# A two-block transformer kernel: branch projections by seven products per pair of output tiles

## The reference

```python
branches = jnp.stack([o_a, o_b, o_c, o_d], axis=2)                       # [1, 512, 4, 512]
up = jnp.einsum("bsnc,ncd->bsnd", branches, w_branch[l])                 # w_branch[l]: [4, 512, 1024]
gates = jax.nn.sigmoid((h @ w_gate[l]).reshape(bsz, seq, N_BRANCH, D_MODEL))
mix = jnp.einsum("bsnd,bsnd->bsd", gates, up) @ w_o[l]
x = x + rms_norm_2(mix, norm_mix_post[l])
```

## Time and profile before

| | us |
|---|---|
| median of 3 runs | 4093.86 |
| the profiled execution, whole | 4087.29 |
| its span, first to last instruction | 4085.5 |
| TensorE busy | 3939.4 (96%) |
| VectorE busy | 2078.0 (51%) |
| GpSimd busy | 1321.1 (32%) |
| ScalarE busy | 828.2 (20%) |

### The profile page before, as it was taken

One profiled execution on the slowest core, in us unless ns is written; L12 is line 12 of the kernel. 1 busy time (PEld: TensorE's weight loads), 2 busy tenths in 40 slices (PEclk: granted clock), 3 DMA queues, 4 the chain that ended last, 5 costly groups with the idle time before them and its releaser, 6 DMA issues. The chain is left out here.

```text
span 4085.5 us, 56674 instructions
## 1 busy us (share of the span) xinstructions
PE 3939.4 (96%) x21187; PEld 3094.6 (76%) x21187; DVE 2078.0 (51%) x3906; ACT 828.2 (20%) x1862; POOL 1321.1 (32%) x1044
## 2 busy tenths in 40 slices
PE   7997999999998999999999999999999999999998
PEld 3886768887886688866688648888666887478887
DVE  3776344423653333225648336884364486257852
ACT  2442310002333100014401202111143201011110
POOL 1333224443320244421146102454311372004543
PEclk8999999999998999999999999999999999999999
DMA  7322234325341233362233231332522233313322
GB/s 240 77 62 94 67 110 130 86 85 162 110 124 39 80 87 84 92 128 41 53 79 89 72 92 52 90 85 85 114 62 65 55 84 82 93 42 93 87 83 77
DMA packets 623320, 360.86 MB, mean 88 GB/s; under 512 B 69083, under 2 KB 592764, under 8 KB 622629
## 3 DMA queue, kind: packets, MB, share of 16 engines
q1 hardware_dynamic: 607960, 335.62, 30.5%
q10 hardware_dynamic: 15180, 22.80, 1.7%
HBM read 344.21 MB, written 6.82 MB: 86 GB/s over the span
## 5 line engine op out<-in xcount | busy, mean ns | idle before, releaser
L851 PE MATMUL psum<-h_normed,weight_slot 128*128 128x256 f32 x2624 | 593.8, 379 | 0.0
L851 PEld LDWEIGHTS psum<-h_normed,weight_slot 128*128 128x128 f32 x2624 | 498.6, 190 | 68.6 <-issue 1.0
L759 POOL TENSOR_TENSOR weight_slot<-weight_slot 128x512 f32<-128x512 f32 (+1 forms) x130 | 170.7, 1313 | 879.5 <-DMA weight_slot<-in_w_ffn_in 292.1
L951 DVE COPY work<-psum 128x256 f32<-128x256 f32 x98 | 41.3, 422 | 592.5 <-PE psum L851 592.4
L3630 PE MATMUL psum<-sums_of_h,weight_slot 128*128 128x256 f32 x1280 | 282.8, 379 | 0.0
L3630 PEld LDWEIGHTS psum<-sums_of_h,weight_slot 128*128 128x128 f32 x1280 | 243.2, 190 | 33.1
L851 PE MATMUL psum<-sums_hidden,weight_slot 128*128 128x256 f32 x1056 | 243.7, 379 | 0.5 <-POOL weight_slot L765 0.5
L851 PE MATMUL psum<-sums_in,weight_slot 128*128 128x256 f32 x1008 | 231.3, 379 | 0.0
L851 PE MATMUL psum<-sums_of_h,weight_slot 128*128 128x256 f32 x960 | 220.5, 379 | 3.7 <-POOL weight_slot L765 3.7
L4522 DVE SCALAR_TENSOR_TENSOR u<-raw,vectors,u 128x511 f32<-128x511 f32 (+1 forms) x160 | 192.2, 1221 | 60.1 <-ACT u L4494 48.4
L3630 PE MATMUL psum<-h_normed,weight_slot 128*128 128x256 f32 x960 | 217.6, 383 | 5.2 <-PEq L209 5.2
(11 more groups left out here) (605 smaller groups left out, 7018.7 us busy)
## 6 DMA issues: line engine op xcount, KB each, us to landing
weight_slot<-in_w_ffn_in SPq DMA_DIRECT2D x88, 512.0 KB
weight_slot<-in_ffn_w_up SPq DMA_DIRECT2D x88, 512.0 KB
weight_slot<-in_w_gate SPq DMA_DIRECT2D x64, 512.0 KB
weight_slot<-in_w_in SPq DMA_DIRECT2D x40, 512.0 KB, 5.4
weight_slot<-in_dsw_w_in SPq DMA_DIRECT2D x36, 512.0 KB, 6.6
weight_slot<-in_gdn_w_in SPq DMA_DIRECT2D x32, 512.0 KB, 14.5
weight_slot<-in_w_ffn_out SPq DMA_DIRECT2D x64, 256.0 KB
tile_ahead<-in_w_ada SPq DMA_DIRECT2D x16, 1024.0 KB, 5.3
```

What stands on the lines that cost most here:

```text
L759: nc.gpsimd.tensor_tensor(b(self.S1), b(self.A21), b(self.A22), ALU.add).then_inc(self.folded, 1)
L851: last = nc.tensor.matmul(c.ps[:, 4 * bank + r // 2, (r % 2) * self.HALF:(r % 2 + 1) * self.HALF], c.slots[s][:, b * 512 + k * P:b * 512 + ...
L951: nc.vector.tensor_copy(u4, p(self.P1)).then_inc(self.link, 1)
```

## The change

Instead of 8 output tiles, `merge_branches` runs 16 steps: 4 pairs of output tiles (i and i + 4) by 4 branches, in the branch order 0, 3, 2, 1. Each step is a 2 x 2 block product with half a branch's depth (256 channels) and half the positions (256) to a block, by seven products; a product has 2 k-tiles. The steps are written out, not looped.

- Folds S2 to S4 are made like S1 in the diff below, each waiting for the one before it; the input sums t2 = b22 - t1, t3 = b22 - b12 (in place of b12) and t4 = b21 - t2 follow t1 in one chain too.
- Weights: 4 buffers of half a slot; two DMAs of 256 KB a step. The first two loads are issued at the end of `conv_pool_gates`, where one of 1 MB was.
- GpSimd: folds each step's weights (4 operations, 128 x 256), makes the input sums (4 operations, 128 x 512) of branches 0 and 3 at the end of `conv_pool_gates` together with the first two folds, those of branch 2 in `merge_branches`, and adds each gated branch to the sum of its pair (2 operations, 128 x 512), 11 of the 12 times.
- VectorE: input sums of branch 1, seven operations per step to combine, two products with the gates, and the last pair of additions.
- ScalarE: copies P1 in each step.
- w_o is loaded in four pairs of tiles as buffers come free, and the first two half products leave k-tiles 3 and 7 for the end.
- New room: `made` (two pairs of tiles) and `work`; input sums lie in `shared` and in `c.h`.

```diff
-def conv_pool_gates(c, layer, o_conv, o_pool, gates, sums_in):
+def conv_pool_gates(c, layer, o_conv, o_pool, gates, sums_in, early):
...
+        ahead = BranchProducts(c, c.next_sems(), early, None)
...
         @block.gpsimd
...
             pool.sem_inc(pooled, 1)
+            pool.wait_ge(done, 2 + SEVEN)
+            for b in EARLY:
+                ahead.sum_inputs(pool, nc.gpsimd, b)
+            for n in range(2):
+                ahead.fold(pool, n)
...
         @block.sync
...
             sp.wait_ge(done, STEPS + 1)
-            sp.dma_start(branch_tile(c, 0), branch_weights(c, layer, 0)).then_inc(c.next_sems()[LOAD0], 16)
+            for n in range(2):
+                ahead.load(sp, layer, n)
...
+BRANCHES = (0, 3, 2, 1)
+EARLY = BRANCHES[0:2]
+
+class BranchProducts(SevenSteps):
+    KB = BW // 2
+    BUFFERS = 4
+    STEPS = KT // 2 * len(BRANCHES)
...
+    def buffer(self, n):
+        m = n % self.BUFFERS
+        at = (1 - m % 2) * (SLOT // 2)
+        return self.c.slots[m // 2][:, at:at + SLOT // 2]
...
+    def fold(self, pool, n):
+        b = lambda j: self.block(n, j)
+        pool.wait_ge(self.loaded[n % self.BUFFERS], 32 * (n // self.BUFFERS + 1))
+        nc.gpsimd.tensor_tensor(b(self.S1), b(self.A21), b(self.A22), ALU.add).then_inc(self.folded, 1)
+        pool.wait_ge(self.folded, 4 * n + 1)
...
+    def sum_inputs(self, engine, on, b):
+        b11, b12, b21, b22 = self.quarters(b)
+        t1, t2, t4 = (self.operands[b][1][:, j, :, :] for j in range(3))
+        on.tensor_tensor(t1, b12, b11, ALU.subtract).then_inc(self.summed[b], 1)
...
+    def multiply(self, pe, n):
...
+        pe.wait_ge(self.loaded[n % self.BUFFERS], 32 * (n // self.BUFFERS + 1))
+        if n >= 2:
+            pe.wait_ge(self.combined, 4 * n - 4)
+        for r, weights, name in ORDER:
+            if r == self.P6:
+                pe.wait_ge(self.folded, 4 * n + 4)
+                if n < len(BRANCHES):
+                    pe.wait_ge(self.summed[b], 4)
+            for k in range(BW // P // 2):
+                last = nc.tensor.matmul(c.ps[:, 4 * (n % 2) + r // 2, (r % 2) * self.HALF:(r % 2 + 1) * self.HALF],
+                                        self.block(n, weights)[:, k * P:(k + 1) * P], self.operand(b, name, k),
+                                        start=(k == 0), stop=(k == BW // P // 2 - 1))
...
 def merge_branches(c, layer, operands, gates, late_room):
...
         @block.gpsimd
...
+            def add_branch(n):
+                if n % NB == 0:
+                    return
+                before = 2 * (n - n // NB - 1)
+                pool.wait_ge(gated, 2 * n + 2)
+                if before:
+                    pool.wait_ge(added, before)
+                for g in range(2):
+                    sum_ = gates[:, n // NB + g * (KT // 2), :]
+                    nc.gpsimd.tensor_tensor(sum_, sum_, made[:, n % 2, g, :], ALU.add).then_inc(added, 1)
+
+            seven.fold(pool, 2)
+            seven.sum_inputs(pool, nc.gpsimd, BRANCHES[2])
+            seven.fold(pool, 3)
+            for n in range(1, STEPS):
+                add_branch(n - 1)
+                if n + 3 < STEPS:
+                    seven.fold(pool, n + 3)
             tail.add_pool(pool, range(KT))
...
         @block.scalar
...
+            for n in range(STEPS):
+                seven.copy_first(act, n)
...
         @block.sync
+            for n in range(2, STEPS):
+                if n >= seven.BUFFERS:
+                    sp.wait_ge(seven.done, n - seven.BUFFERS + 1)
+                seven.load(sp, layer, n)
+            for buffer, q in enumerate((0, 2, 1, 3)):
+                sp.wait_ge(seven.done, STEPS - seven.BUFFERS + buffer + 1)
+                for n in (2 * q, 2 * q + 1):
+                    sp.dma_start(out_tile(c, n), layer_columns(c.ins["w_o_2"], layer, n * P, P)).then_inc(out_loaded[q], 16)
...
         @block.tensor
...
+            for n in range(STEPS):
+                seven.multiply(pe, n)
...
+            LAST_MADE = (KT // 2 - 1, KT - 1)
+            READY = tuple(k for k in range(KT) if k not in LAST_MADE)
+            pe.wait_ge(out_loaded[0], 32)
+            pe.wait_ge(seven.combined, 4 * (STEPS - 1))
+            product(0, READY)
+            product(1, READY)
+            product(0, LAST_MADE)
+            product(1, LAST_MADE)
...
         @block.vector
+            seven.sum_inputs(dve, nc.vector, BRANCHES[3])
+            for n in range(STEPS):
+                i, b = n // NB, BRANCHES[n % NB]
+                if n >= 2 and (n - 2) % NB:
+                    dve.wait_ge(added, 2 * (n - 2 - (n - 2) // NB))
+                seven.combine_step(dve, n, made[:, n % 2, 0, :], made[:, n % 2, 1, :])
+                dve.wait_ge(seven.combined, 4 * n + 4)
+                for g in range(2):
+                    tile, gate = made[:, n % 2, g, :], gates[:, i + g * (KT // 2) + b * KT, :]
+                    nc.vector.tensor_tensor(tile if n % NB else gate, tile, gate, ALU.mult).then_inc(gated, 1)
...
```

More of the change, by code:

```diff
@@ L4216, in out_tile, with merge_branches @@
     return c.slots[n // 2 % 2][:, at:at + D].rearrange("p (k n) -> p k n", k=KT)
-def merge_branches(c, layer, branches, gates, part, late_room):
+def merge_branches(c, layer, operands, gates, late_room):
     nc = c.nc
-    NB, CT, HS = 4, BW // P, S // 2
+    NB, HS = len(BRANCHES), S // 2
     LATE, FIRST = range(KT // 2, KT), range(KT // 2)
     ORDER = tuple((0, n) for n in range(KT)) + tuple((1, n) for n in LATE) + tuple((1, n) for n in FIRST)
-    with c.stage(square=[P, 2, 3, HS], total=[P, 3, HS], diagonal=[P, 2, HS]) as (block, sems, square, total, diagonal):
-        loaded, done, freed, gated, dve_link = sems[0:2], sems[2], sems[3], sems[4], sems[5]
-        kept, taken, squared, crossed, summed, out_near, out_far, next_cleared = sems[6:14]
-        LINKS = 3
+    with c.stage(square=[P, 2, 3, HS], total=[P, 3, HS], diagonal=[P, 2, HS], work=[P, 3, HS], made=[P, 2, 2, S]) as (
+            block, sems, square, total, diagonal, work, made):
+        done, freed, gated = sems[2:5]
+        kept, taken, squared, crossed, summed, next_cleared, added = sems[6:13]
+        out_loaded = sems[43:47]
+        seven = BranchProducts(c, sems, operands, work)
+        STEPS = seven.STEPS
         YY, XZ, ZZ = range(3)
@@ L4273, in _ @@
         def _(sp):
-            def load_out(n):
-                sp.dma_start(out_tile(c, n), layer_columns(c.ins["w_o_2"], layer, n * P, P)).then_inc(out_near if n in FIRST else out_far, 16)
-            for n in range(1, KT):
-                sp.wait_ge(done, n + 1)
-                sp.dma_start(branch_tile(c, n % 2), branch_weights(c, layer, n)).then_inc(loaded[n % 2], 16)
-                if n == 3:
-                    for m in FIRST:
-                        load_out(m)
-            for n in LATE:
-                sp.wait_ge(done, KT + 1 + (n // 2) % 2)
-                load_out(n)
+            for n in range(2, STEPS):
[6 more added lines that the diff above has]
+                    sp.dma_start(out_tile(c, n), layer_columns(c.ins["w_o_2"], layer, n * P, P)).then_inc(out_loaded[q], 16)
             sp.wait_ge(next_cleared, 1)
@@ L4294, in _ @@
         def _(pe):
-            pe.sem_inc(done, 2)
-            with pe.Fori(0, KT // 2) as i:
-                for s in range(2):
-                    pe.wait_ge(loaded[s], i * 16 + 16)
-                    pe.wait_ge(freed, i * 2 + (s + 1))
-                    for b in range(NB):
-                        for k in range(CT):
-                            last = nc.tensor.matmul(c.ps[:, 4 * s + b, :], c.slots[s][:, (b * CT + k) * P:(b * CT + k + 1) * P],
-                                                    branches[b][:, k, :], start=(k == 0), stop=(k == CT - 1))
-                    last.then_inc(done, 1)
+            pe.sem_inc(done, 2 + KT)
+            for n in range(STEPS):
+                seven.multiply(pe, n)
             def product(j, ks):
@@ L4310, in product @@
                     if j < 2:
-                        pe.wait_ge(freed, k + 3)
+                        pair = k % (KT // 2)
+                        if pair < KT // 2 - 1:
+                            pe.wait_ge(added, 2 * (NB - 1) * (pair + 1))
+                        else:
+                            pe.wait_ge(freed, k // (KT // 2) + 1)
                     last = nc.tensor.matmul(y(j), out_tile(c, n)[:, k, :], gates[:, k, q * HS:(q + 1) * HS],
@@ L4315, in product @@
                     last.then_inc(done, 1)
[L4317 to L4322 removed]
+            LAST_MADE = (KT // 2 - 1, KT - 1)
[6 more added lines that the diff above has]
+            product(1, LAST_MADE)
             for j in range(2, 2 * KT):
[L4324 to L4325 removed]
+                if j < KT and j % 2 == 0:
+                    pe.wait_ge(out_loaded[j // 2], 32)
                 pe.wait_ge(taken, j - 1)
@@ L4565, in second_block @@
             gates = sb("branch_gates", [P, 32, S])
```

(7 more changed lines are left out.)

82 lines of the change are left out of this document (54 added, 28 removed).

## The result

The changed kernel takes 4053.12 us (median of 4, 4050.78 to 4055.59) beside 4093.05 us (4086.2 to 4094.44) for the kernel before on the same chip: ratio 0.991 [0.9898, 0.9922], 0.9% faster. The profiled execution took 4050.78 us where that of before took 4087.29.

What follows compares the result with a forecast made beforehand. TensorE, busy 96%, was taken as the bound: 13.2 us a layer from fewer products plus 0.4 at w_o, 27.2 us for two layers, giving 4060.1, or 4066.7 us on the median's scale; range 4061 to 4079.

Steps and rivals of the forecast that it cites:

- TensorE's work: Branch products: 16 steps of 28 records at 0.2158 us, 6.04 us a step, 96.7 us a layer before the clock term.
- I keep the 1.80 us of clock, since the idle ahead of the stage stays: Start of the branch products: the clock falls after the unchanged idle, costing 1.80 us, so the stage takes 98.5 us.
- I take 0: Start of the branch products: writing the loop out costs TensorE nothing; bounds 0.6 us more to 2 us less a layer.
- that execution lay 6.6 us under the median: Whole program: profiled 4087.3 us against median 4093.9, so the forecast 4060.1 was moved to 4066.7 us.
- GpSimd: Branch products: last weight fold ends at 87.9 us with contention, wanted at 94.2, 6 us of slack.
- A: Branch products: every GpSimd operation contested, factor 1.25, last fold 4.1 us late; 4071 to 4081 us; chance 0.09.
- A': Branch products: each VectorE product stops GpSimd for all its 0.69 us, last fold 2 us late; 4071 us; chance 0.05.
- B: Branch products: GpSimd becomes the bound, slower; 4112 us at factor 1.5, some 4155 at 1.79; chance 0.06.
- Against: POOL's loses 0.34 us there and no more: Argument against A': beside VectorE's two-input operations, GpSimd's operation loses only 0.34 us, not the full 0.69.
- Step 2: Third step of the branch products, tightest GpSimd deadline: input sums done at 14.5 us, wanted at 15.6.
- The junction with w_o: From branch products to w_o: four records left to the end cover TensorE's stop, 0.4 us gained a layer.
- C, no change: Branch products: GpSimd factor near 1.38, or 1.8 us half-clock periods after short waits in seven or more steps; near 4090; chance 0.04.

Runs made afterwards that it cites:

- the late start: Changed kernel with TensorE's first product of the stage held until VectorE's first input sum is done: 4058.8 us, stages 98.45 and 98.46 us.

## Why the prediction missed

**TensorE's work: right.** 28 records in 6.04 us, 16 times: 96.7 forecast from the earlier trace rows, 96.77 measured. This is the term that makes the change: (109.95 - 96.77) = 13.18 us a layer at equal clock, 26.4 of the gain.

**"I keep the 1.80 us of clock, since the idle ahead of the stage stays": wrong, the step of the mechanism that failed, worth 3.4 of the 13.6 us by which the forecast was high.** The idle did not stay: 1.62 us instead of 1.95. That 0.33 us is small as time and large as condition: the clock stayed up, worth 1.7 us a layer, 3.4 in all. Put back, it gives the forecast stage (98.45 us in the late start). The block ahead does end the same way; the block that follows doesn't begin the same way.

**"I take 0" for writing the loop out: wrong by 0.33 us a layer.** I had bounds of +0.6 and -2 us and took the middle on the argument of the wait at another stage's start (2.6 us). Writing out alone gives 1.95 to 1.77 us; what gives the last 0.15, down to 1.62, I have not isolated. It equals the 0.15 us that one more signal on TensorE cost; but the changed stage gives as many signals as the written-out one and drops the wait for free banks instead, so that the same 0.15 us stands behind it is only argued. The bound of up to 2 us less was the place to ask: less idle, and then what does the clock do? Forecasting 3.4 + 0.7 us more would have given 4062.6, just inside the range.

**The scale and the range: too narrow, and more than half of the miss.** The remaining 9.5 us to the measured median, 4062.6 to 4053.1, are neither stage nor start. I moved the forecast from one profiled execution to a median by a constant ("that execution lay 6.6 us under the median") and allowed nothing for how executions differ. Executions of the kernel before run from 4077.53 us (mean clock 0.986) to 4104.18, and one of 4099.86 has 0.981. Over all sets, chips mixed, 56 executions of before average 4091.1 us and 16 of the changed kernel 4055.6: a difference of 35.4 (95%: 2.9 either way). That is 4.5 less than the medians of the first sets of four showed, so this part of the miss is chance in which executions were taken, and 4.9 more than the 30.5 of the stages and starts. Span times mean clock, a measure of work at full clock, is 4021.0 (the 51 executions of the larger sets) against 3992.8: 28.2 (standard error 1.0), where the terms of work are 2 x 13.18 + 0.8 + 0.7 = 27.9. So the work is accounted for. What is left is clock, 7.1 us less lost with a standard error of 2.1, of which the stage explains at most 3.4. The other 3.7 us lie in shared code and are less than two standard errors: that the change saves clock outside its stage is not shown, and why one execution loses more there than another is open.

**GpSimd: right in sum, by terms that cancel.** Forecast 87.9 us for the last fold, measured 86.4. The first load was there 3.5 us after TensorE's start in the first layer, not 5.2 (half a megabyte, was for one), and an early pair of additions took 3.27 us, not 2.7: it stands beside VectorE's products. A contested operation loses 0.33 us (0.72 to 1.05, 1.27 to 1.60), as taken from the earlier trace rows, or more, up to 0.53. Slack 6.0 for the 6.3 forecast, and the two kernels with more work on GpSimd gave the price of overrunning it. One term was missing: the fold of step 4 stands ahead of the additions of step 1, so these ended at 23.3 us, not "20.4 at the latest", and VectorE waited 1.3 us for them. Rivals A, A' and B fell on this: A would have the last fold at 98.3 us, A' at 96.3.

**"Against: POOL's loses 0.34 us there and no more": the reading that dismissed A' was wrong about the mechanism.** The rows fit one engine being held fully while the other works. Five operations of the first layer, GpSimd's and VectorE's by turns, each begun while the one before it still ran:

```profile
2341.21 0.73 POOL L4257 TENSOR_TENSOR weight_slot<-weight_slot 128x256 f32<-128x256 f32 x1
2341.54 0.94 DVE L4464 TENSOR_TENSOR made<-made,branch_gates 128x512 f32<-128x512 f32 x1
...
2342.01 1.60 POOL L4361 TENSOR_TENSOR branch_gates<-branch_gates,made 128x512 f32<-128x512 f32 x1
...
2342.41 1.76 DVE L4464 TENSOR_TENSOR made<-made,branch_gates 128x512 f32<-128x512 f32 x1
...
2343.58 1.71 POOL L4361 TENSOR_TENSOR branch_gates<-branch_gates,made 128x512 f32<-128x512 f32 x1
```

Each of the four later ones ends where the one before it ends, less 0.14 us, plus its own time alone (0.69 or 1.27 us): 2341.94 - 0.14 + 0.69 = 2342.49 for a measured 2342.48, then 2343.61, 2344.16 and 2345.30 for 2343.61, 2344.17 and 2345.29. So end all 103 operations of GpSimd and products of VectorE in the two layers that began while the other engine's was more than 0.14 us from its end, to 0.01 us. This also gives the 0.33 us: in a chain GpSimd begins its next operation 0.08 us after the end of the last, 0.22 us after VectorE's waiting product was let go, and waits for the rest, 0.69 - 0.14 - 0.22 = 0.33 us. A product of VectorE's that comes early in one of GpSimd's operations loses more, up to 1.07 us. One fold operation that began 0.01 us behind a product took 1.26 us for 0.73. The rule in the Trainium skill ("SBUF — State Buffer", section "Who interferes with whom") is that the second to come blocks fully, and the trace agrees but for the 0.14 us. A' had the mechanism right and its price too high, 0.69 us for each product.

**Step 2: the tightest deadline, as forecast, and a little over it in one layer.** I had 14.5 us for the sums against 15.6 wanted; with the clock up TensorE comes 1.7 us earlier, at 13.9. Layer 1 makes it, because its first load was there at 3.5 us: its sums end at 12.7. In layer 2 the load was there at 5.0 us, nearly the 5.2 I took, and the sums end at 14.4, nearly the 14.5: 0.52 us late at TensorE, and 0.76 us in the length of the stage. A gain in one place had eaten the slack in another, which my sum had kept apart.

**VectorE: covered, but not for free.** In the first layer it waited five times for GpSimd's additions; all of it lay beside TensorE's work:

```profile
DVE made L948 <- POOL branch_gates L4361: 6.5, 5, 1.3
```

**The junction with w_o: right.** 0.41 us a layer, gone; from first to last of its 256 records w_o is 0.36 us shorter. **C, no change:** fell; no short wait inside the stage dropped the clock.

## What to carry to other kernels

A stage's start is a condition of the clock as well as a wait: read the granted clock behind it, and where an edit shortens or lengthens the wait by tenths, price both levels. Work moved to an idle engine is free until a deadline: write the deadline of each operation and the slack, here 6 us in 92, which half an operation more per fold would use. Where two engines meet in SBUF, ask which begins first: the later one waits for the other's end. When one profiled execution is set beside a median, take the spread of executions and their mean clock into the range.

## What the runs showed of the hardware

- The clock after a short idle, at the start of one stage of one program: none of 18 starts after 1.62 or 1.77 us fell, 9 of 10 after 1.92 to 2.31 us did, at 1.7 us each. Elsewhere the length alone does not decide: 1.37 us among small products was followed by the 1.2 GHz level, and one stop of 2.45 us and 18 of at most 0.9 us within dense products were not.
- With the loops written out, a block's first matmul began after 0.18 us less idle, twice; with one more signal ahead of it on TensorE, after 0.15 us more, twice.
- Where GpSimd and VectorE both read two inputs from SBUF, the later one ends 0.14 us less than its own time alone after the earlier one's end (103 of 103, to 0.01 us). The price differs by side: GpSimd's 128 x 256 operation goes from 0.72 to 1.05 us, at most 1.26, and VectorE's 128 x 512 product from 0.69 to 1.14 us on average in 22, at most 1.76. Taking 22 additions a layer from GpSimd brought that average to 0.80.
- A stop costs more than the idle time that the trace shows: in the kernel with two extra operations 10.8 us of waits (0.5 of them for the input sums) lengthened the stage by 15.4 us, about 0.25 us more for each of 18 stops. 0.16 of that is how records are counted: a 256-wide record lasts 0.38 us and the next starts 0.216 us after it did, so idle time begins to count 0.16 us late. The first record behind a stop lasts 0.08 us longer.
